# Gate and up products of a SwiGLU FFN as seven half-size products (Strassen's scheme, 2x2 quarters) instead of eight

## The reference

```python
gate, up = jnp.split(rmsnorm(x, norm_ffn[l]) @ ffn_w_gu[l], 2, axis=-1)   # w_gu: 1024 x 5632
x = x + (jax.nn.silu(gate) * up) @ ffn_w_down[l]                          # w_down: 2816 x 1024
return rmsnorm(x, norm_final)
```

## Time and profile before

| what | value |
|---|---|
| median of 3 runs | 1750.23 us (1747.47 to 1753.62) |
| the profiled execution | 1744.98 us |
| its span (first to last instruction) | 1743.2 us |
| PE busy | 1671.4 us, 96% of the span |
| mean granted TensorE clock | 0.991 |
| FFN part, from the last norm tile to the end | about 1026 to 1743 us |

### The profile page before, as it was taken

One profiled execution on the slowest core, in us unless ns is written; L12 is line 12 of the kernel. 1 busy time (PEld: TensorE's weight loads), 2 busy tenths in 40 slices (PEclk: granted clock), 3 DMA queues, 4 the chain that ended last, 5 costly groups with the idle time before them and its releaser, 6 DMA issues.

```text
span 1743.2 us, 31883 instructions
## 1 busy us (share of the span) xinstructions
PE 1671.4 (96%) x13513; PEld 1380.5 (79%) x13513; DVE 715.2 (41%) x1212; ACT 661.6 (38%) x1239; POOL 576.3 (33%) x534
## 2 busy tenths in 40 slices
PE   6999999999967999899999999999999999999998
PEld 5888878779755878678898888888888888888886
DVE  3104888244375765553514621311311311311316
ACT  5224888542365544334545732111111111111113
POOL 5222664211155633265462032222222222222220
PEclk9999999999989999999999999999999999999999
DMA  6110000211000010035241021111111111111112
GB/s 200 47 48 26 1 1 2 97 36 43 19 0 7 5 52 5 4 129 210 85 134 54 1 73 49 49 43 55 49 43 55 49 43 55 49 43 54 49 43 97
DMA packets 63036, 91.62 MB, mean 53 GB/s; under 512 B 5058, under 2 KB 46176, under 8 KB 62640
## 3 DMA queue, kind: packets, MB, share of 16 engines
q1 hardware_dynamic: 61952, 87.08, 15.3%
q0 software_dynamic: 944, 2.52, 0.5%
HBM read 83.29 MB, written 6.29 MB: 51 GB/s over the span
## 4 chain that ended last, share of the span: by engine, by line
PE 90%; DVE 4%; ACT 3%; DMA 2%; issue 1%; POOL 0%; SPq 0%; ACTq 0%; DVEq 0%
PE PS L1684 14%; PE PS L1685 14%; PE PS L1687 14%; PE PS L1965 7%; PE PS L2339 4%; PE PS L2337 4%; PE PS L2338 4%; PE PS L1697 4%; PE PS L1699 4%; PE PS L1698 4%; PE PS L1789 3%; PE PS L1833 3%; PE PS L2037 2%; PE PS L1825 1%; PE PS L1723 1%
## 5 line engine op out<-in xcount | busy, mean ns | idle before, releaser
L494 POOL TENSOR_TENSOR WL<-RAW,WH 128x512 fp32r<-128x512 f32 x248 | 338.6, 1375 | 857.6 <-ACT WH L685 857.3
L1684 PE MATMUL PS<-HH,WH 128*128 128x512 f32 x1040 | 407.5, 392 | 0.3 <-DVE SM L1175 0.3
L1685 PE MATMUL PS<-HL,WH 128*128 128x512 f32 x1040 | 404.7, 389 | 0.0
L685 ACT ACTIVATE WH<-RAW 128x512 fp32r<-128x512 f32 x248 | 153.5, 631 | 540.5 <-PE PS L1687 231.0
L1687 PE MATMUL PS<-HH,WL 128*128 128x512 f32 x1040 | 325.5, 389 | 0.0
L1684 PEld LDWEIGHTS PS<-HH,WH 128*128 128x128 f32 x1040 | 195.3, 188 | 41.0 <-issue 0.7
L1687 PEld LDWEIGHTS PS<-HH,WL 128*128 128x128 f32 x1040 | 195.2, 188 | 40.7
L1685 PEld LDWEIGHTS PS<-HL,WH 128*128 128x128 f32 x1040 | 195.3, 188 | 40.6 <-issue 0.7
L1634 DVE TENSOR_TENSOR FU<-PS,ACTB 128x512 f32<-128x512 f32 x44 | 27.3, 684 | 456.9 <-PE PS L1687 456.9
L2337 PE MATMUL PS<-WH,AH 128*128 128x512 f32 x352 | 136.9, 389 | 0.0
L2338 PE MATMUL PS<-WL,AH 128*128 128x512 f32 x352 | 136.9, 389 | 0.0
(11 more groups left out here) (350 smaller groups left out, 2662.7 us busy)
## 6 DMA issues: line engine op xcount, KB each, us to landing
RAW<-in_ffn_w_gu SPq DMA_DIRECT2D x88, 256.0 KB, 2.8
RAW<-in_w_in SPq DMA_DIRECT2D x48, 256.0 KB, 2.9
RAW<-in_ffn_w_down SPq DMA_DIRECT2D x44, 256.0 KB, 2.6
RAW<-in_w_out SPq DMA_DIRECT2D x32, 256.0 KB, 2.8
XT<-in_x SPq DMA_DIRECT2D x8, 512.0 KB, 5.3
X<-in_x SPq DMA_DIRECT2D x8, 512.0 KB, 6.5
RAW<-in_x_wq SPq DMA_DIRECT2D x16, 256.0 KB, 2.7
RAW<-in_x_wkv SPq DMA_DIRECT2D x16, 256.0 KB, 2.6
```

The lines of the kernel that those rows point to most:

```text
L494: pool.tensor_tensor(w_low, RAW[:, p % NRAW], w_high.bitcast(F32), ALU.subtract).then_inc(w_lo, 1)
L685: act.activation(split_at(p)[0], RAW[:, p % NRAW], ACT.Copy).then_inc(w_hi, 1)
L1684: pe.matmul(where(ct, i), wh[:, k, c], ah(kt)[:, t0:t0 + n], start=first and starts(ct, i), stop=False, skip_group_check=True)
L1685: pe.matmul(where(ct, i), wh[:, k, c], al(kt)[:, t0:t0 + n], start=False, stop=False, skip_group_check=True)
```

## The change

The gate and up products of rounds 1 to 10 are made by Strassen's scheme in Winograd's form (7 products). For one kind (gate or up) of one round the weight is split into quarters: A11, A12 (the two halves of the contraction for features 0 to 127), A21, A22 (for features 128 to 255). The tokens are halved too: B11, B21 (contraction halves of tokens 0 to 511), B22 and B12 for the other tokens. Each result cell C11, C12, C21, C22 is 128 features x 512 tokens. Round 0 and the down jobs are made as before, with the same number of matmuls.

- **Inputs.** Once, after the last norm tile, DVE makes four sums T1 to T4 of input quarters (8 operations of 128 x 2048), ACT rounds them (`t_round`, 4 x 128 x 2048) and DVE makes their low parts (`t_low`, 4 x 128 x 2048). T3 takes the place of B12 in `HH` and `HL`, so ACT must wait with it until the first two pieces of up in round 0 are used.
- **Weights.** Each kind's 1024 x 256 weights of a round are loaded whole (two DMAs of 512 KB, `load_set`) into `WSET`. POOL makes S1 to S4 (`sums`, four operations of 128 x 512, in place, the four on one another). An operand (a quarter or a sum) of 128 x 512 goes through the slots as a piece did: 14 per round and 4 for down, instead of 12.
- **Products.** A product is 4 x 3 = 12 matmuls of 512 columns. Several products share a bank: PE adds the next one onto the last, and ACT copies the partial sum out in between (`keep`, three per kind, counted by `f_s`). DVE adds three cells per kind (`cell`, counted by `f_cell`); C21 is left complete in its bank.
- **Order.** On PE: G A11, then U A22 and U S4 of the round before, the down job of the round before, G A12, S2, S1, S3, U A11, G A22, G S4, U A12, S2, S1, S3. The down job reads `FH` and `FL`. Their last cells (C21 after U A22, C12 after U S4) are complete only just ahead of it, where before the down job was one round behind.
- **Down weights.** They have two buffers `WD_RAW0/1`: the load of piece (1, k) waits until POOL is done with piece (0, k).
- **Banks.** The down job uses banks in the order `DOWN_BANKS`; a tile waits for the addition of the tile that had its bank, five or more tiles before.
- The gain of the final norm is loaded after the last U A22.

The core of the diff (`sums` is POOL's, the loop with `hi` and `keep` ACT's, `up_ends` DVE's, run ahead of the down tiles' additions, and `product` PE's):

```diff
+            operands += down
+            if i < FF_ITERS:
+                operands += [("G", i, m) for m in ("A12", "S2", "S1", "S3")]
+                operands += [("U", i, "A11"), ("G", i, "A22"), ("G", i, "S4")]
+                operands += [("U", i, m) for m in ("A12", "S2", "S1", "S3")]
...
+        DOWN_BANKS = (1, 2, 3, 7, 6, 4, 5, 3, 7, 6, 4, 5, 3, 7, 6, 4)
...
+            def load_down(i, h):
+                for k in range(2):
+                    if h or i:
+                        last = PLACE["D", i, (0, k)] if h else PLACE["D", i - 1, (1, k)]
+                        sp.wait_ge(w_hi, last + 1)
+                        sp.wait_ge(w_lo, last + 1)
+                    sp.dma_start(WDN[k][:, :], w_dn[i * PW + k * P:i * PW + k * P + P, 512 * h:512 * h + 512]).then_inc(down_in[k], 16)
...
+            def sums(kind, i):
+                pool.wait_ge(w_lo, used_by(kind, i, "A12"))
...
+                pool.tensor_tensor(a11, a11, a21, ALU.subtract).then_inc(s_sum, 1)
+                pool.wait_ge(s_sum, summed(kind, i, "S3"))
+                pool.tensor_tensor(a21, a21, a22, ALU.add).then_inc(s_sum, 1)
+                pool.wait_ge(w_used, s2 - NW + 1)
+                pool.tensor_tensor(quarter(kind, i, "S2"), a22, a11, ALU.subtract).then_inc(s_sum, 1)
+                pool.wait_ge(s_sum, summed(kind, i, "S2"))
+                pool.tensor_tensor(a12, a12, quarter(kind, i, "S2"), ALU.subtract).then_inc(s_sum, 1)
...
+            for i in range(1, FF_ITERS):
+                first = PLACE["D", i - 1, (0, 0)]
+                hi(first + 4)
+                if i > 1:
+                    product_hi(i - 1, 2, "C22")
+                    product_hi(i - 1, 3, "C21")
+                hi(first + 5)
+                if i > 1:
+                    product_hi(i - 1, 4, "C12")
+                hi(first + 8)
+                keep("G", i, "A11")
+                hi(first + 10)
+                silu(i, "C11")
+                hi(first + 11)
+                keep("G", i, "S2")
+                hi(first + 13)
+                keep("G", i, "S3")
+                hi(first + 14)
+                keep("U", i, "A11")
...
+                hi(first + 19)
+                keep("U", i, "S3")
+                hi(first + 20)
...
+            def up_ends(i):
+                gated(i, "C21")
+                product_lo(i, 2, "C22")
+                product_lo(i, 3, "C21")
+                cell("U", i, "C12")
+                gated(i, "C12")
+                product_lo(i, 4, "C12")
...
+            def product(kind, i, name):
...
+                for k in range(4):
+                    pe.matmul(dst, wh[:, k], bh[:, k], start=start and k == 0, stop=False, skip_group_check=True)
+                    pe.matmul(dst, wh[:, k], bl[:, k], start=False, stop=False, skip_group_check=True)
+                    mm = pe.matmul(dst, wl[:, k], bh[:, k], start=False, stop=k == 3, skip_group_check=True)
+                mm.then_inc(w_used, 1)
...
+                pe.wait_ge(f_s, g + 3)
+                pe.wait_ge(t_lo, 4)
+                product("G", i, "A22")
```

More of the change, by code:

```diff
@@ L150, in build @@
         GBF = at("GBF", 34.5, [D])
-        GBL = at("GBL", 200, [D])
+        GBL = at("GBL", 172, [D])
         MX = at("MX", 180, [2, D])
@@ L1109, in _, with t_round @@
                     hi(N_LIN + 4)
[L1111 to L1127, removed]
+            def t_round(dst, src, n):
+                act.wait_ge(t_sum, n)
+                act.activation(dst, src, ACT.Copy).then_inc(t_hi, 1)
@@ new lines, in _, with silu @@
+            hi(N_LIN + 12)
+            act.wait_ge(t_lo, 3)
+            t_round(QTR_R[3][:, :, :], QTR[4][:, :, :], 8)
+            hi(N_LIN + 13)
+            for k in range(4):
+                c = slice(512 * (k % 2), 512 * (k % 2) + 512)
+                act.wait_ge(f_mul, k + 1)
+                act.activation(FH[:, k // 2, c], GATE[:, k // 2, c], ACT.Copy).then_inc(f_hi, 1)
+            def silu(i, name):
+                f, c = CELLS[name]
+                if name == "C21":
+                    act.wait_ge(w_used, used_by("G", i, "A22"))
+                    src = PS[:, 0, :]
+                else:
+                    act.wait_ge(f_cell, 3 * pair("G", i) + ADDED.index(name) + 1)
+                    src = GATE[:, f, c:c + 512]
+                act.activation(GATE[:, f, c:c + 512], src, ACT.Silu).then_inc(f_silu, 1)
@@ L1129, in _ @@
+            last = FF_ITERS - 1
+            hi(N_ALL)
+            product_hi(last, 2, "C22")
+            product_hi(last, 3, "C21")
+            product_hi(last, 4, "C12")
             for tt in range(NT):
@@ L1624, in final @@
                 STT(FO[:, tt % 2], X[:, tt], FR[:, tt:tt + 1], GBL[:, :], ALU.mult, ALU.mult).then_inc(l_o, 1)
[L1626 to L1661, removed]
@@ new lines, in _, with cell @@
+            for n, name in ((1, "C11"), (3, "C21"), (2, "C12"), (4, "C22")):
+                product_lo(0, n, name)
+            def cell(kind, i, name):
+                dst, a = (GATE, 0) if kind == "G" else (UP, 4)
+                f, c = CELLS[name]
+                product, kept, bank = {"C11": ("A12", 1, a + 2), "C22": ("S1", 3, a + 1), "C12": ("S4", 2, a + 1)}[name]
+                dve.wait_ge(w_used, used_by(kind, i, product))
+                dve.wait_ge(f_s, 3 * pair(kind, i) + kept)
+                TT(dst[:, f, c:c + 512], PS[:, bank, :], dst[:, f, c:c + 512], ALU.add).then_inc(f_cell, 1)
@@ new lines, in _ @@
+            for i in range(1, FF_ITERS):
+                if i > 1:
+                    up_ends(i - 1)
+                for n in range(16):
+                    add_down(i - 1, n)
+                for name in ADDED:
+                    cell("G", i, name)
+                cell("U", i, "C11")
+                gated(i, "C11")
+                product_lo(i, 1, "C11")
+                cell("U", i, "C22")
+                gated(i, "C22")
+            last = FF_ITERS - 1
+            up_ends(last)
+            dve.wait_ge(gain_in["final"], 16)
@@ new lines, in _ @@
+            last = FF_ITERS - 1
+            pe.wait_ge(f_s, 3 * pair("U", last) + 3)
+            product("U", last, "A22")
+            pe.wait_ge(f_cell, 3 * pair("U", last) + 2)
+            product("U", last, "S4")
+            ws = [wide_piece() for _ in range(4)]
+            for tt in range(NT):
+                for h in range(2):
+                    n = 2 * tt + h
+                    down_ready(last, n, tt)
+                    for k in range(2):
+                        mm = down_mm(DOWN_BANKS[n], *ws[2 * h + k], k, tt)
+                    mm.then_inc(f_mm, 1)
```

382 lines of the change are left out of this document (305 added, 77 removed).

## The result

| | before | changed |
|---|---|---|
| median | 1750.74 us (1747.47 to 1753.62, 4 runs) | 1725.61 us (1723.69 to 1732.64, 4 runs) |
| profiled execution, and its span | 1744.98 and 1743.2 us | 1724.45 and 1722.7 us |
| mean granted clock | 0.991 | 0.984 |

The ratio is 0.9864 (95% interval 0.9831 to 0.9898): 1.4% faster, and the median lies 0.1 us from the predicted 1725.7. The interval is 12 us wide, so a match that close is luck; what can be judged is each term. By the medians the gain is 25.1 us.

A forecast was written before the change was run, and what follows sets the result against it. The prediction took TensorE's matmuls to bound each round. It summed -54.4 for products, +17.9 for down-job stalls, +8.6 for the start gap and +3.4 for the clock to -24.5 us: 1725.7 us, range 1703 to 1745.

The forecast's parts named there:

- The products: Gate and up in 10 rounds: 2 x 84 instead of 2 x 96 matmuls each, saving 54.4 us.
- Chain A: Middle of a round, up sums and roundings until G A22: covered by three products, price 0, 0.4 us to spare.
- My bound of 0.45 per round: Ahead of G A22: price in us per round if POOL's sums cost 1.36 us like low parts.
- my signs of being wrong: Down-job wait nil or over 3 us, POOL sums clearly over 1.1 us, or clock below 1.00 in the rounds.
- Chain B: Ahead of the down job, from the end of U S3 to C21's low part: stall of 1.9 us in 9 rounds.
- The last round: Ahead of the last down job: no G A12, VectorE goes at once, so the stall is 0.8 us.
- The gap at the start: Ahead of the first down job: TensorE stalls 8.6 us behind VectorE's input sums, roundings and low parts.
- The clock at the start: Behind the gap at the start: 6.8 us at half clock speed lose 3.4 us.
- The end: Last down job: VectorE makes good its lag of about 2.5 us, the gain's load lands in time; price 0.
- Chains covered: Rival: the chains beside the products are covered, 1699 to 1709 us; chance 0.2.
- The load is late: Rival: load of down piece (1, 1) is late, or chain A not covered; 1740 to 1752 us; chance 0.15.
- The clock falls in every round: Rival: TensorE's clock falls behind each down-job gap, costing 34 us more, 1760 us; chance 0.08.

The follow-up runs named there:

- first edit: Against the changed kernel, ACT rounds cells C22 and C21 ahead of down pieces (1, 0) and (1, 1); 1702.76 us.
- Both repairs: Against the changed kernel, cells rounded ahead of the late down pieces, and at the start T4's rounding and low part put behind the products'; 1698.61 us.
- shorter gap: Against the kernel with both repairs, C11 and C21 are multiplied and lowered first at the start, and the first down tiles wait for these alone; 1699.15 us.
- doubled sum: Against the changed kernel, POOL makes the sum S2 of each up weight twice; 1734.85 us.
- third experiment: Against the changed kernel, the rounding of the next G A12 moves behind that of cell C12; 1713.2 us.
- first two: Each against the changed kernel: cells C22 and C21 rounded ahead of the late down pieces, 1702.76 us; down piece (0, 1) rounded ahead of the copy of U S3, 1705.29 us.

## Why the prediction was right

The sum as it came out in the FFN part: -54.4 + 9 x 2.0 + 1.5 + 7.65 + 2.9 + 1.0 + 0.7 = -22.65, against -22.5 measured. Term by term:

- **The products, -54.4.** Right. The nearest proof is the period of 59.84 us with the first edit, where no wait is left. Both repairs together bring the FFN part 48.4 us below that of before (717.0 - 668.6), with the shorter gap 51.3 (717.0 - 665.7), so nearly all of the forecast gain is there once the waits are gone.
- **Chain A, 0 with 0.4 to spare.** Right, though two sizes in it were off and cancelled. POOL's sums take 1.28 us, not 1.09: the plain fp32 sum of the earlier trace rows was the wrong row. So the `keep` of G S3 ends at 1110.21, 7.88 us after the end of G S2 (1102.33, by the `keep` at 1102.53), and not after 7.5. With the 0.3 that I had put between it and TensorE that is 8.18, and all the cover of 8.16 is used. But G A22 starts right on time, without a wait, and the doubled sum shows 0.4 still to spare: the 0.3 was too much. My bound of 0.45 per round for slow sums therefore did not come. That sums take clearly more than 1.1 us, and that the clock is below 1.00 in a round, were two of my signs of being wrong. Both came true, at no cost for the first and 1.5 us for the second. POOL's and ACT's timelines, and TensorE's:

```profile
1105.08 1.28 POOL L761 TENSOR_TENSOR WU_RAW<-WU_RAW 128x512 f32<-128x512 f32 x1
1106.44 1.28 POOL L763 TENSOR_TENSOR WU_RAW<-WU_RAW 128x512 f32<-128x512 f32 x1
1107.68 1.29 POOL L765 TENSOR_TENSOR SLOT_F<-WU_RAW 128x512 f32<-128x512 f32 x1
...
1102.53 0.60 ACT L1296 ACTIVATE GATE<-PS 128x512 f32<-128x512 f32 x1 [0.84 <-PE PS L2612]
...
1109.63 0.58 ACT L1296 ACTIVATE GATE<-PS 128x512 f32<-128x512 f32 x1
```

```profile
1110.49 0.39 PE L2610 MATMUL PS<-QTR_R,WH 128*128 128x512 f32 x1
```

- **Chain B, 1.9 in nine rounds and 0.8 in the last.** Right in mechanism and size: 1.66 to 1.86 of wait and 0.3 of restart. Counted from the end of U S3 (1126.81, 0.20 before the `keep`), piece (0, 1) is lowered at 2.69 (forecast 2.75), the load lands at 5.42 (5.43), POOL ends its second operation at 9.21 (9.16), VectorE at 9.77 (9.72), and TensorE goes on at 10.01 (10.0). The third experiment takes the second meeting out alone, and the first two show that the chain runs from the `keep` of U S3 to the cells. I had not foreseen the other way that it takes in two rounds. Without meetings I had put 0.1 per round, which by my own rows is 0.26 (6.76 + 2 x 0.69 + 0.28 - 8.16); this touches a rival, not the sum.
- **The last round, 0.8.** Wrong in place, right in size. The wait does not stand ahead of the last down job, because there piece (0, 1) is rounded early; TensorE waits 0.69 us two products earlier, at U A22, for ACT's copy of U S3. With no G A11 in between, nothing covers that copy. I had written "in the last there is no G A12" and not looked at what else is missing.
- **The gap at the start, 8.6.** 7.65 us (TensorE idle from 1064.65, the end of its last up matmul's slot, to 1072.30). TensorE's end and the multiplications (1067.77) both came 2.0 us after their forecast times, 1062.6 and 1065.8, as the last norm tile did. On the way two errors cancelled: the eight sums took 21.4 us (1028.28 to 1049.67) and not 24, since fewer of POOL's operations fell among them, and the load of piece (1, 0), behind the up weights, took 5.03 us and not 2.6. The gap is 1 us shorter than the sum since no POOL operation fell among the three low parts that the down job waits for (1.81 us).
- **The clock at the start, 3.4.** TensorE worked 5.8 us at half speed (1072.30 to 1078.12, by the windows below): 2.9. That is close by chance: with gaps of 6.7 to 7.0 us, four other kernels worked 3.6 to 5.7 us at half speed. The clock fell 3.1 us after the last matmul's record ended (1064.82 to 1067.88); in the earlier trace rows it is 3.3 (1734.64 to 1737.90, where I had read 1734.62 and 1737.95).

```profile
1067.00:1068.00 1.00, 0.00 (x0) 0.00 (x0) 1.00 (x2) 0.00 (x0) 1.00 (x1) 0.94 0.21 80
...
1078.00:1079.00 1.00, 1.00 (x6) 0.83 (x5) 0.49 (x1) 0.20 (x1) 0.86 (x2) 0.94 0.00 0
```

- **The end, 0.** The span ends 9.65 us after the start of the last matmul (1722.7 - 1713.05) and not 8.95 (1743.2 - 1734.25): 0.7 us.

The rivals. *Chains covered*: no, there were waits of 15.7 us in the rounds. *The load is late*: where the chain runs through it, in seven rounds, the load of piece (1, 1) took 2.63 to 2.81 us. It was piece (1, 0) that came late, in two rounds, where it cost at most 0.2 us each, and at the start, where the shorter sums offset it. (10 x 2 us more than my sum is 1746; the 1740 in this rival's range did not follow from it.) *The clock falls in every round*: in one of nine, which costs 1.5 us, not 34. I had ruled it unlikely by the 3.3 us of idle time in the earlier trace rows; that argument does not hold, for it fell behind a wait of 1.83 us here and behind 2.55 and 2.3 in experiments. The sum did not rest on this argument, but the rival's small chance did.

The meetings of POOL and VectorE carry nearly all of the wait: 1.15 us of it left with the second one, and the 0.58 that stayed is what two low parts take beyond 2 x 0.69 us when only the first is left. The rule that I took from the Trainium skill ("SBUF — State Buffer", Who interferes with whom), that the two exclude each other, agrees with these two numbers; who goes first when both wait came from the rows alone.

## What to carry to other kernels

A scheme that saves matmuls shortens the cover of all that runs beside them, and makes inputs due at once that used to be a round old: follow each of these inputs back to the buffer and the last load that stand ahead of it in its engine's order. Of the 54 us saved here 30 went to two such orders (18 + 1.5 for the cells behind a load, 7.65 + 2.9 for the input sums); rounding the cells first and the last sum's low part later gave 26 to 27 of them back (1725.6 to about 1699 us, 2.9% below the kernel before). Price a new operation by a row with the same layout and output type, not merely of the same size, as long as it isn't shown which of these sets its time.

## What the runs showed that I had not expected

- **The clock after short gaps.** At the start of the FFN it fell to 1.2 GHz behind waits of 2.55 and 2.3 us, for 3.4 us each time, and stayed up behind 1.0, in one profiled execution of each kernel. In the rounds, three kernels have waits of about 1.7 us ahead of nine down jobs each; behind those 27 it fell twice (here and with the doubled sum), and in the rounds of the kernels without them never. Each such fall costs about 1.5 us. The two waits were of 1.83 and 1.99 us, the other 25 of 1.54 to 1.95, so the length alone does not decide; what sets the two apart stays open.
- **POOL's sums.** 1.28 to 1.29 us for 128x512 from the weight set, against 1.09 in the earlier trace rows. Both are fp32 in SBUF, so the layout is the suspect; that was not tried by itself.
- **VectorE's long sums beside POOL.** The first four of 128x2048, during which POOL makes three low parts, take 12.09 us, the next four without POOL 9.27: 2.8 us for three operations. POOL pays too, with 4.59 us for two:

```profile
1028.01 4.59 POOL L571 TENSOR_TENSOR WL<-RAW,WH 128x512 fp32r<-128x512 f32 x2 [4.26 <-ACT WH L831]
1032.97 2.92 POOL L571 TENSOR_TENSOR WL<-RAW,WH 128x512 fp32r<-128x512 f32 x1 [0.38 <-ACT WH L831]
```

- **Identical code, different pace.** The stretch ahead of the FFN ended between 1026.2 and 1035.1 us over nine kernels that do the same work there. A single span can mislead by several us, which is why the FFN part was used.
